# Down projection of the gated MLP as a Strassen product: seven block products for eight, its weight combinations formed during the up projection and kept in DRAM

## The reference

```python
def conv_gated_mlp(x, w_up, conv_w, conv_b, w_down):
    h = x @ w_up                                  # 1024 -> 2 x 2816
    ...                                           # 3-tap convolution along the tokens
    a, gate = jnp.split(h, 2, axis=-1)
    return (jax.nn.silu(gate) * a) @ w_down       # 2816 -> 1024
...
    f = conv_gated_mlp(x, w_up[l], conv_w[l], conv_b[l], w_down[l])
    x = layer_norm(DEEPNORM_ALPHA * x + f, ln2_g[l], ln2_b[l])
```

## Time and profile before

| | |
|---|---|
| median of 3 runs | 3188.85 us |
| the profiled execution | 3188.99 us, its span 3187.2 us |
| TensorE busy | 3040.2 us, 95% of the span |
| VectorE, ScalarE, GpSimd busy | 1958.7, 1132.2, 646.5 us |
| up projection | 1475 to 2570.5 us of the span |
| down projection | 2571.3 to 3169.9 us: 2640 matmuls |
| DMA | 251 GB/s over the span, at most 336 in a fortieth of it |

### The profile page before, as it was taken

One profiled execution on the slowest core, in us unless ns is written; L12 is line 12 of the kernel. 1 busy time (PEld: TensorE's weight loads), 2 busy tenths in 40 slices (PEclk: granted clock), 3 DMA queues, 4 the chain that ended last, 5 costly groups with the idle time before them and its releaser, 6 DMA issues.

```text
span 3187.2 us, 43463 instructions
## 1 busy us (share of the span) xinstructions
PE 3040.2 (95%) x15920; PEld 2591.7 (81%) x15920; DVE 1958.7 (61%) x3210; ACT 1132.2 (36%) x2092; POOL 646.5 (20%) x582
## 2 busy tenths in 40 slices
PE   6999998896999998999999999999999999999997
PEld 4777766665677776888999999999999988888886
DVE  7637745753767756668667584675656564464464
ACT  2247445522344433224333341332323343232231
POOL 0012101003554320322232331323222200000000
PEclk9999999998999999999999999999999999999999
DMA  7889788857886856898787887878899874545542
GB/s 272 319 286 305 245 284 262 280 182 247 262 277 232 261 205 207 284 336 302 254 298 236 270 290 228 283 241 262 276 303 333 292 264 158 189 171 181 188 172 93
DMA packets 362865, 799.16 MB, mean 251 GB/s; under 512 B 37632, under 2 KB 145552, under 8 KB 362656
## 3 DMA queue, kind: packets, MB, share of 16 engines
q1 hardware_dynamic: 350016, 743.36, 70.4%
q0 software_dynamic: 12640, 53.04, 4.6%
HBM read 625.20 MB, written 175.18 MB: 251 GB/s over the span
## 4 chain that ended last, share of the span: by engine, by line
PE 57%; DVE 3%; issue 1%; DMA 1%; POOL 0%; ACT 0%; ACTq 0%; DVEq 0%; POOLq 0%
PE trunk_ps L77 19%; PE trunk_ps L76 19%; PE trunk_ps L78 19%; DVE trunk_h L2196 1%; DVE trunk_h L2191 0%; PE trunk_ps L2397 0%; DVE trunk_h L2178 0%; DVE trunk_stats L2186 0%; DVE shared_ring L2238 0%; DMA shared_ring<-xop 0%; POOL trunk_x1t L1951 0%; DMA xop<-trunk_tt 0%; DVE trunk_tt L2210 0%; DMA xop<-trunk_p 0%; DVE shared_ring L2210 0%
## 5 line engine op out<-in xcount | busy, mean ns | idle before, releaser
L76 PE MATMUL trunk_ps<-shared_ring 128*128 128x512 f32 (+2 forms) x1136 | 423.9, 373 | 8.3 <-PEq L1072 5.4
L77 PE MATMUL trunk_ps<-shared_ring 128*128 128x512 f32 (+2 forms) x1136 | 422.6, 372 | 0.0
L78 PE MATMUL trunk_ps<-shared_ring 128*128 128x512 f32 (+2 forms) x1136 | 421.2, 371 | 0.0
L76 PE MATMUL trunk_ps<-shared_ring,trunk_w_rest 128*128 128x426 f32 (+2 forms) x816 | 302.5, 371 | 5.8 <-issue 5.6
L77 PE MATMUL trunk_ps<-shared_ring,trunk_w_rest 128*128 128x426 f32 (+2 forms) x816 | 303.2, 372 | 0.0
L78 PE MATMUL trunk_ps<-shared_ring,trunk_w_rest 128*128 128x426 f32 (+2 forms) x816 | 301.7, 370 | 0.0
L2092 ACT ACTIVATE trunk_tt<-trunk_h,trunk_cw 128x851 f32<-128x851 f32 (+2 forms) x132 | 136.1, 1093 | 388.5 <-DVE trunk_h L2270 360.4
L76 PE MATMUL front_acc<-shared_ring 128*128 128x512 f32 x640 | 262.1, 409 | 8.8 <-ACT front_out L578 8.8
L78 PE MATMUL front_acc<-shared_ring 128*128 128x512 f32 x640 | 253.5, 396 | 0.0
L77 PE MATMUL front_acc<-shared_ring 128*128 128x512 f32 x640 | 253.2, 396 | 0.0
L76 PEld LDWEIGHTS trunk_ps<-shared_ring 128*128 128x128 f32 x1136 | 214.2, 189 | 31.4 <-issue 7.4
(11 more groups left out here) (221 smaller groups left out, 6352.6 us busy)
## 6 DMA issues: line engine op xcount, KB each, us to landing
shared_ring<-xt_s SPq DMA_DIRECT2D x280, 512.0 KB, 6.6
shared_ring<-xop SPq DMA_DIRECT2D x312, 426.0 KB, 4.1
shared_ring<-xop SPq DMA_DIRECT2D x168, 428.0 KB, 5.1
shared_spare<-in_w_down SPq DMA_DIRECT2D x110, 512.0 KB, 3.4
shared_spare<-in_w_up SPq DMA_DIRECT2D x198, 256.0 KB, 5.6
trunk_s<-g_s SPq DMA_DIRECT2D x110, 256.0 KB, 3.6
xt_s<-shared_ring SPq DMA_DIRECT2D x40, 512.0 KB, 5.8
front_region<-in_x SPq DMA_DIRECT2D x20, 512.0 KB, 9.1
```

Source lines behind the costliest of these rows:

```text
L76: pe.matmul(out, lh, rh, start=first, stop=False, skip_group_check=skip)
L77: pe.matmul(out, lh, rl, start=False, stop=False, skip_group_check=skip)
L78: return pe.matmul(out, ll, rh, start=False, stop=last, skip_group_check=skip)
```

## The change

The product f = g·W_down is cut in 2x2 blocks: rows in two tiles of 128 tokens (a pair), the 22 chunks in two halves of `KH = 11`, and the 1024 columns in two halves. Strassen's form (Winograd's variant) needs seven block products for eight.

- **W side.** For each of 11 chunks, four quads of `w_down` are loaded through the six quad slots, POOL forms t3, t2, t4 and t1 in place (`combine_down`), ACT and DVE split all seven operands into two halves of the buffer `s2` ("emits", two in turn), and SP stores each (512 KB) to the new scratch `wop`. A chunk takes three steps of the up projection, with 3, 2 and 2 emits, at `CHUNK_TAGS`. An emit may be written when the store two before it has landed.
- **A side.** 70 visits: 2 halves of the tokens (five pairs each) x 7 products x 5 pairs ("lanes", one PSUM bank each). A visit loads one to three blocks of 128x1408 of `g_s` (704 KB, in pieces of 512 B; "raws", 90 in all, four buffers), adds them on DVE where the product is of a sum (`visit_combine`), splits the result (`visit_hi`, `visit_lo`, three buffers) and runs 11 x 3 matmuls. Product 2 (s2, visits 10 to 14 and 45 to 49) needs three raws a visit.
- **The stored W** comes back as 154 loads of 512 KB, 11 for each product, 15 buffers; a buffer is free when the last lane has used it.
- **Results.** DVE adds each bank to the rows it belongs to, which begin as x1 (`visit_take`); rows are normalised and stored after products 5 and 6.

```diff
+EMITS = ("t3", "b11", "b22", "b21", "t2", "t4", "t1")
+EMIT_AT = ((0, 3), (3, 5), (5, 7))
+CHUNK_TAGS = (9, 25, 30, 46, 51, 67, 72, 88, 93, 109, 114)
+DLANES, DHALVES, WUNITS, ABUFS, RAWA = 5, 2, 15, 3, 4
...
+            if v % DLANES == DLANES - 1:                              # visit_done
+                eng.wait_ge(wd_used, KH * (v // DLANES + 1))
...
+                eng.wait_ge(wd_used, u - WUNITS + 1)                  # down_w_free, u >= 15
...
+                visit_done(eng, v - ABUFS)                            # a_free, v >= 3
...
+                    elif kind == "down":                              # load_quad
+                        sp.wait_ge(wd_lo, k)
...
+            def store_emit(number):
+                c, e, _, out = emit_of(number)
+                sp.wait_ge(wd_lo, number + 1)
+                sp.dma_start(wop[DOWN_W.index(EMITS[e]), c], out).then_inc(wd_stored[number % 2], 16)
...
-            def load_unit(d):
...
+            def load_w(u):
...
+                down_w_free(sp, u)
+                sp.dma_start(down_w(u).bitcast(F32), wop[phase % PHASES, k]).then_inc(wd_in[u % WUNITS], 16)
+
+            def load_raw(r):
+                v, pair, kh, row = raws[r]
+                if r < 2:
+                    sp.wait_ge(w_lo, len(items))
+                    sp.wait_ge(wd_lo, PHASES * KH)
+                elif r < RAWA:
+                    sp.wait_ge(xq_used, 4 * NSTEP_UP)
                 else:
+                    prior = raws[r - RAWA][0]
+                    if DOWN_A[prior // DLANES % PHASES] == "s2":
+                        sp.wait_ge(a_comb, comb_by[prior])
+                    else:
+                        sp.wait_ge(a_lo, prior + 1)
...
+                    if 1 <= j <= len(emits_at(n)):                    # SP, step n, after load_x and load_quads
+                        store_emit(emits_at(n)[j - 1])
+                if n > LAST_SB and n - LAST_SB - 1 < 4:
+                    for u in range(*((0, 3), (3, 7), (7, 11), (11, 15))[n - LAST_SB - 1]):
+                        load_w(u)
+                if n == LAST_SB + 5:
+                    for r in range(2):
+                        load_raw(r)
...
+            for v in range(NVISIT):                                   # SP
+                while loaded < len(raws) and raws[loaded][0] <= v + 3:
+                    load_raw(loaded)
+                    loaded += 1
+                if v == 1:
                     sp.wait_ge(carried, len(convs))
                     for l in range(LANES):
                         sp.wait_ge(g_stored[l], 16 * sum(cl == l for _, cl in convs))
...
+                    for l in range(2, DLANES):
+                        load_rows(0, l)
...
+                if v % DLANES == DLANES - 1:
+                    first = KH * (v // DLANES) + WUNITS
+                    for u in range(first, min(first + KH, DHALVES * PHASES * KH)):
+                        load_w(u)
...
+            def emit_hi(number):                                      # ACT; emit_lo on DVE alike
...
+                need(act, wd_stored[number % 2], 16 * (number // 2))
+                act.activation(out[:, 0:HALF].bitcast(F32R), quad_of(quad_no), ACT.Copy).then_inc(wd_hi, 1)
...
+            def visit_combine(v):                                     # DVE
...
+                if op == "s2":
...
+                    dve.tensor_tensor(total, raw_a(own[0]), raw_a(own[1]), ALU.add).then_inc(a_comb, 1)
+                    dve.wait_ge(a_comb, comb_by[v] - 1)
+                    dve.tensor_tensor(total, total, raw_a(own[2]), ALU.subtract).then_inc(a_comb, 1)
...
+            def visit_lo(v):
+                dve.wait_ge(a_hi, v + 1)
+                dve.tensor_tensor(a_buf(v)[:, 1], a_source(v), a_buf(v)[:, 0].bitcast(F32), ALU.subtract).then_inc(a_lo, 1)
...
+                if n == NSTEP_UP:                                     # DVE, end of step n, after the convolutions
+                    visit_lo(1)
+                    visit_lo(2)
+                if n == NSTEP_UP - 1:
+                    visit_lo(0)
+            for v in range(1, NVISIT + 1):
+                if 3 <= v + 2 < NVISIT:
+                    visit_lo(v + 2)
+                visit_take(v - 1)
+                if v + 3 < NVISIT:
+                    visit_combine(v + 3)
+                for row in {5: (1,), 6: (0,)}.get((v - 1) // DLANES % PHASES, ()):
+                    down_norm(v - 1, row)
...
+            def visit(v):                                             # TensorE
...
+                pe.wait_ge(a_lo, v + 1)
...
+                    if l == 0:
+                        pe.wait_ge(wd_in[u % WUNITS], 16 * (u // WUNITS + 1))
...
+                    mm = three_pass(pe, ps[:, bank, :], (a_of[:, 0, cols], a_of[:, 1, cols]),
+                                    (w_of[:, 0, :], w_of[:, 1, :]), k == 0 and fresh, k == KH - 1, not fresh)
```

More of the change, by code:

```diff
@@ L1475 @@
 VIA_MEMORY = (34, 36)
-BLOCKS = (4, 3, 2, 1, 0)
 GROUP0 = 3
@@ L1544, in trunk @@
     quad_order = []
+    chunk_quads = []
+    for c in range(KH):
+        chunk_quads.append([len(quads) + j for j in range(4)])
+        quads += [(c, (1, 1), "down", 7 * c + 7), (c, (0, 1), "down", 7 * c + 7), (c, (0, 0), "down", 7 * c + 5),
+                  (c, (1, 0), "down", 7 * c + 6)]
     for tag in tags:
+        if tag in CHUNK_TAGS:
+            quad_order += [(tag, number) for number in chunk_quads[CHUNK_TAGS.index(tag)]]
         for k in sum_at.get(tag, []):
@@ L1880, in _, with load_rows @@
+            def load_rows(half, l):
+                for row in range(2):
+                    t = 2 * l + row
+                    if half:
+                        sp.wait_ge(y_stored[t], 16)
+                    sp.dma_start(y_rows[t], x1[rows_of(2 * DPAIRS[half][l] + row), :]).then_inc(x1_in[t], 16)
             for kc in range(M_EARLY, KC):
@@ L2010, in _ @@
                     sum_w(k)
+                c, step = chunk_step(n)
+                if c is not None:
+                    combine_down(c, step)
                 if n == 2:
@@ new lines, in visit_lo, with visit_take @@
+            def visit_lo(v):
+                dve.wait_ge(a_hi, v + 1)
+                dve.tensor_tensor(a_buf(v)[:, 1], a_source(v), a_buf(v)[:, 0].bitcast(F32), ALU.subtract).then_inc(a_lo, 1)
+            def visit_take(v):
+                half, at = divmod(v, PHASES * DLANES)
+                phase, l = divmod(at, DLANES)
+                src = ps[:, DBANK[l], :]
+                low, high = slice(0, HALF), slice(HALF, D)
+                upper, lower = y_rows[2 * l], y_rows[2 * l + 1]
+                visit_done(dve, v)
+                if phase < 2:
+                    for row in range(2):
+                        dve.wait_ge(x1_in[2 * l + row], 16 * (half + 1))
+                    for part in ((upper[:, high], lower[:, low], lower[:, high]) if phase == 0 else (upper[:, low],)):
+                        dve.scalar_tensor_tensor(part, part, ALPHA, src, ALU.mult, ALU.add).then_inc(d_read, 1)
+                    return
+                dve.wait_ge(d_read, read_by[v - DLANES])
+                part = (upper[:, high], lower[:, high], lower[:, low], lower[:, high], upper[:, high])[phase - 2]
+                dve.tensor_tensor(part, part, src, ALU.add).then_inc(d_read, 1)
@@ L2484, in _ @@
                 phase(n)
[L2485 to L2498 removed]
+            for v in range(NVISIT):
+                visit(v)
 def encoder(nc, a, y_all):
```

371 lines of the change are left out of this document (228 added, 143 removed).

## The result

The changed kernel takes 3248.23 us (median of 4 runs, 3240.59 to 3248.93) against 3188.62: ratio 1.0183, 95% interval 1.0166 to 1.0201, 59.6 us slower. The forecast was 3183 (3140 to 3218): wrong in sign, and outside its range. The profiled execution's span is 3247.1, 59.9 more than before.

What follows compares the result with a forecast made beforehand. TensorE's matmuls were taken to bound the kernel, in the down projection for 598.62 of 598.70 us. A gain of 75.4 less costs of 69.2 made net -6.2 from 3189: 3183 us, range 3140 to 3218.

Steps and rivals of the forecast that it cites:

- matmuls, tail: Down projection and tail: 330 fewer matmuls save 74.8 us, one eviction less in the tail saves 0.6.
- Step 1: Up projection: chunks' quads and stores delay x loads, dearest at chunk 93 (8.5); +20 us, ends 4 and 39.
- Step 2: Turn between projections: up projection ends 4.3 late, then late raw 0 and visit 1's late low part; +14.3 us.
- 3, visit 5: Visit 5: SP's hold at visit 1 for the last g delays raw 5, W stands behind raws; +6.6 us.
- Step 4: Visits 10-14 and 45-49: three raws in four buffers, W behind waiting raws; +12.9 and +10.4 us.
- Step 5: Products 5 and 6: DVE needs 8.1 us a visit against 7.48; +5 us, ends 0 and 5.
- the 40 named as a sign of being wrong: Up projection: the prediction is wrong if it lengthens by less than 5 us or more than 40.
- the prediction's cycle of landing and adding: s2 visits: two raw transfers, landing and two adds take 9.9 us against 7.48, losing 2.4 per visit.
- The rival that DVE bounds products 5 and 6 at full price: Products 5 and 6: normalisation waits in every visit, 15 to 20 us for 5, total 3195; chance 0.10.
- The rival of late raws: s2 visits: raws landing 12 us after release lose 7.7 per visit instead of 2.4, total 3215; chance 0.22.
- a landing above 8 us: Raw loads: a raw landing after more than 8 us was named as showing the prediction wrong.
- The rival that the loads keep up: Down projection: raws arrive in time, leaving costs of 25 us in the whole kernel, total 3139; chance 0.25.

Runs made afterwards that it cites:

- e12: Changed kernel with two emit buffers, one outside s2, so the next pass's sum waits for the sixth emit's store or none: 3229.36 us, ratio 1.0124.
- e1: Changed kernel with a third emit buffer; the next pass's weight sum waits only for the store whose place it overwrites: 3208.98 us, ratio 1.0052.
- e3: Changed kernel with the split of visit 1 moved ahead of the last block's convolutions: 3246.6 us, ratio 1.0163.
- e5: Changed kernel with each raw loaded from one chunk in 5632 B pieces instead of 512 B (wrong values): 3218.82 us, ratio 1.0087.
- e14: As e11, with five of product 2's eleven W loads ahead of the raws that wait for a combine: 3161.49 us, ratio 0.9915.
- e10: Changed kernel with g_s kept in tiles: raws load in 5632 B pieces, POOL writes in 512 B or less: 3214.15 us, ratio 1.0081.
- e11: Changed kernel with three emit buffers, three reorderings of loads, hold and split at the turn, and tiled g_s together: 3166.22 us, ratio 0.9927.
- e13: As e11, with the W loads of all products after the first issued by POOL instead of SP: 3205.57 us, ratio 1.005.

## Why the prediction was wrong

| step | forecast | measured |
|---|---|---|
| matmuls, tail | -75.4 | -74.8, tail +4.3 |
| 1, up projection to step 121 | +20 | +53.0 |
| 2, its end, the turn, visits 0 to 4 | +14.3 | +21.0 |
| 3, visit 5 | +6.6 | +4.2 |
| 4, s2 visits | +23.3 | +35.6 |
| 5, products 5 and 6 | +5 | +6.4 |
| visits 35 and 40 | none | +7.0 |
| start of the up projection | none | +3.3 |

The gain of the matmuls was right to a microsecond; the costs were 69 where 130.5 came, and the tail, taken as 0.6 shorter, is 4.3 longer.

- **Step 1 failed**, at the sentence "SP is held by the emits at the four that begin beside a block's convolutions: 1.6 each". These four cost 26.1. I saw the pace of the emits but took five quarters of x, 11.7 us, as cover; and I left out a wait that is in the diff's neighbourhood and not in its words: the next pass's sum waits for the last store, because the emits live in the sums' places. That wait is 13.9 of the 26.1 (e12); the rest is the pace together with the sum's wait for the store before. Chunk 93 has the same second wait behind the first: 15.3 for 8.5, of which 3.2 go in e12. The chunks from step 108 on cost 9.9 for 4.5, 4.1 with a third buffer (e1). The lower clock after a gap had no term here and is 9.3 of the 26.1. The bytes, on which half of my working rested, cost nothing with four lanes (e1); with three that is open. The up projection became 63 us longer, beyond the 40 named as a sign of being wrong.
- **Step 2** was right in its mechanisms (late low part of visit 1, W before x) and short by 6.7. The term that was mis-sized is the end of the up projection, 9.9 for 4.3: the third window has 6.7 us without a matmul, and a clock of 0.91 over its 40.1 is some 3.6 more, an estimate. The half clock after the gap before visit 1, which I left out because visit 5 would take it up, is 4.7 of the 9.7 that visits 0 to 4 lose; and it was taken up. Visits 0 to 5 lose 13.9 where the 6.9 and 6.6 of the prediction make 13.5, and with visit 1 in time they lose 13.8 (e3).
- **Step 4** had the cause in part. The long waits stand at visits 10, 12 and 13 (forecast: 10, 13 and 14), with W behind the raws. Two terms were wrong. A raw was priced at 2.25 us, from the 320 to 350 GB/s in the middle of the earlier trace rows; it flows at 290, 2.5 us, as the last third of that row does (262 to 320, but for its last slice). And visit 45 was given 5.2 for the 7.7 of visit 10, since loads would arrive there undelayed; it loses 10.1, as much as visit 10. With 2.5 us a raw the prediction's cycle of landing and adding is 2 x 2.5 + 2.1 + 3.24 = 10.3 us a visit. The sum of bytes, three raws (2.5 each) and 2.2 W (1.28 each), is 10.3 as well. With large pieces the two are 8.8 and 8.1, and visits 11 to 14 lose 0 to 2 each (e5). So which of the two sets the pace is not shown.
- **Step 5** came near its size in the visits, 6.4 for 5, in part by luck: DVE shows at visits 32 and 33 (4.1), and visits 30 and 65 wait for W. With the tail, where DVE comes 4.1 us later than before, its price is some 8. The rival that DVE bounds products 5 and 6 at full price did not come true: most of their visits lose nothing.
- **The rival of late raws** named the right side and a true reading, a landing above 8 us (10.2), which the prediction had as a sign of being wrong. But the landing isn't what costs: with large pieces it rises to 12.7 and the kernel is 29 us faster. Its price, 3215, was not the sum either.
- **The rival that the loads keep up** did not come true, and with the waits of e14 removed the kernel is still at 3161, where it said 3139.
- Visits 35 and 40, without a term in the prediction, wait for W (0.3 to 0.9 us at a time).

The Trainium skill ("DMA: Bandwidth & Descriptors", Specifications) has line rate from 512 B on. The runs disagree, and the measurement decides: 290 GB/s with 512 B, 410 with 5632 B, in the same place (e5).

## What to carry to other kernels

A buffer borrowed from another stage brings that stage's waits with it: before pricing its fill, list who writes there next and what stands behind that writer on every in-order queue. Price a load at the rate at which its own size of piece flows for long (290 here), not at that of the best stretch of a row. And of several late operands, moving the first one up gains nothing until the next, behind its own hold, moves too.

## What the runs showed of the hardware

- Loads in 512 B pieces flow at 290 GB/s, in 5632 B pieces at 410. Stores of the tiled `g_s`, in pieces of 512 B and less, cost the up projection nothing that stands out of its spread (78.6 us lost, 73.2 to 78.5 without them).
- The median landing of a load is no measure of its cost: for raws it rose from 10.2 to 12.7 and 13.0 us while the kernel became 29 and 34 us faster (e5, e10). That they were issued earlier into full queues is likely, but no run shows it by itself.
- After a gap of 4.8 us TensorE ran at a mean granted clock of 0.68 for 6.8 us; the step with this gap lost 7.0 in all.
- POOL's last DRAIN, with no other work left, takes 8.72 us in the kernels before and after (140 DMAs issued by POOL), 2.43 in e10, e11 and e14 (228) and 8.47 in e13 (367). What sets it, no run shows.
